# Gated linear attention: the values of two heads made in one product of 512 columns

## The reference

```
o_intra = where(causal, (q*exp(b)) @ (k*exp(-b)).T, 0) @ v     # by head and chunk
o_inter = (q*exp(b)) @ state;  state = decay*state + (k*exp(b_last-b)).T @ v
o = rmsnorm(o_intra + o_inter) * silu(r)
```

## Time and profile before

| what | value |
|---|---|
| median of 3 runs | 2038.2 us (2037.76 to 2039.65) |
| the profiled execution | 2040.08 us, of which 2038.0 us are the span from the first to the last instruction |
| PE busy | 99% of the span, 10,731 matmuls |
| DVE / ACT / GpSimd busy | 78% / 49% / 19% |
| granted clock of PE, mean | 0.997 |
| chain that ended last | PE 92%, DVE 5%, ACT 1% |

### The profile page before, as it was taken

One profiled execution on the slowest core, in us unless ns is written; L12 is line 12 of the kernel. 1 busy time (PEld: TensorE's weight loads), 2 busy tenths in 40 slices (PEclk: granted clock), 3 DMA queues, 4 the chain that ended last, 5 costly groups with the idle time before them and its releaser, 6 DMA issues.

```text
span 2038.0 us, 28513 instructions
## 1 busy us (share of the span) xinstructions
PE 2013.1 (99%) x10731; PEld 1766.3 (87%) x10731; DVE 1590.8 (78%) x2874; ACT 997.7 (49%) x1684; POOL 384.1 (19%) x298
## 2 busy tenths in 40 slices
PE   9999999999999999999999999999999999999998
PEld 7888888887887888889999999999998888888886
DVE  6799576757977455999898997777577888888886
ACT  6577455544245324434366767777343333333333
POOL 2000200000000001000122222222233444444430
PEclk9999999999999999999999999999999999999999
DMA  7411246341212222125789989999999999999991
GB/s 279 152 54 42 73 152 225 145 166 62 93 63 73 83 89 101 63 93 173 251 289 319 333 304 334 329 325 328 385 365 386 370 373 377 386 386 389 387 381 76
DMA packets 137288, 471.39 MB, mean 231 GB/s; under 512 B 10096, under 2 KB 59760, under 8 KB 111552
## 3 DMA queue, kind: packets, MB, share of 16 engines
q1 hardware_dynamic: 50368, 309.59, 41.4%
q0 software_dynamic: 36864, 134.23, 17.5%
q10 hardware_dynamic: 49920, 25.75, 4.3%
HBM read 416.97 MB, written 52.43 MB: 230 GB/s over the span
## 4 chain that ended last, share of the span: by engine, by line
PE 92%; DVE 5%; ACT 1%; issue 1%; DMA 0%; ACTq 0%; DVEq 0%
PE bank L159 91%; DVE whl L316 1%; DVE L L1593 1%; PE bank L756 1%; DVE L L1591 1%; PE bank L1688 0%; DVE L L1574 0%; PE bank L351 0%; DVE B L1063 0%; ACT whl L309 0%; DMA raw<-in_l_in 0%; DVE wk L2049 0%; DVE L L1979 0%; DVE i L2047 0%; DVE i L2055 0%
## 5 line engine op out<-in xcount | busy, mean ns | idle before, releaser
L159 PE MATMUL bank<-xhl,whl 128*128 128x384 f32 (+1 forms) x5256 | 1058.7, 359 | 8.2 <-DVE whl L316 3.2
L159 PEld LDWEIGHTS bank<-xhl,whl 128*128 128x128 f32 x5256 | 938.9, 189 | 92.2 <-issue 4.4
L316 DVE TENSOR_TENSOR whl<-raw,whl 128x1024 fp32r<-128x1024 f32 (+1 forms) x395 | 469.7, 1199 | 225.0 <-ACT whl L309 213.5
L309 ACT ACTIVATE whl<-raw 128x1024 fp32r<-128x1024 f32 (+1 forms) x395 | 400.7, 1027 | 258.6 <-PE bank L159 250.0
L159 PE MATMUL bank<-whl,ag 128*128 128x512 f32 x2304 | 525.3, 390 | 0.0
L159 PEld LDWEIGHTS bank<-whl,ag 128*128 128x128 f32 x2304 | 431.8, 188 | 89.3
L2406 POOL DMA_INDIRECT row<-in_U_rows,row_at x128 | 153.4, 1198 | 586.9 <-DVE row L2419 426.9
L2406 POOL DMA_INDIRECT row<-in_V_rows,row_at x128 | 186.5, 1457 | 245.7 <-DVE y_tok L2435 215.2
L2435 DVE SCALAR_TENSOR_TENSOR y_tok<-row,row_a,y_tok 128x1024 f32<-128x1024 f32 x127 | 162.5, 1280 | 2.6
L2419 DVE SCALAR_TENSOR_TENSOR row<-row,h_tok 128x1024 f32<-128x1024 f32 x128 | 155.8, 1218 | 3.0 <-DMA row<-in_U_rows,row_at 3.0
L159 PE MATMUL bank<-yhl,whl 128*128 128x512 f32 x636 | 149.6, 390 | 1.6 <-DVE whl L316 1.0
(11 more groups left out here) (300 smaller groups left out, 1834.7 us busy)
## 6 DMA issues: line engine op xcount, KB each, us to landing
raw<-in_U SPq DMA_DIRECT2D x64, 1024.0 KB, 7.4
raw<-in_V SPq DMA_DIRECT2D x64, 1024.0 KB, 7.5
hidden<-h_both SPq DMA_DIRECT2D x32, 768.0 KB, 10.4
gates<-g_stage ACTq DMA_DIRECT2D x12, 2048.0 KB, 24.8
g_ring<-gates SPq DMA_DIRECT2D x32, 768.0 KB, 12.5
h_ring<-hidden SPq DMA_DIRECT2D x22, 768.0 KB, 9.7
raw<-in_w_ada SPq DMA_DIRECT2D x16, 1024.0 KB, 5.6
raw<-in_w_gla SPq DMA_DIRECT2D x12, 1024.0 KB, 4.9
```

What stands on the lines that cost most here:

```text
L159: return e.matmul(o, a, b, start=start, stop=stop, skip_group_check=True)
L309: e.activation(hi[:, s], src[:, s], ACT.Copy).then_inc(act_hi.of((i, half)))
L316: e.tensor_tensor(lo[:, s], src[:, s], F(hi[:, s]), ALU.subtract).then_inc(dve_lo.of((i, half)))
```

## The change

Values are made for two heads at once, in P1 for heads 0 and 1 and in P3 for heads 2 and 3. A value item holds half the contraction (four chunks of X) for both heads' 512 columns, so that a pair takes two items (gla1 then gla4; gla7 then gla10), parts 0 and 1, and 96 matmuls of 512 columns. Four banks, one for each block of 128 tokens, are filled together ahead of the first matmul and stay open over both parts. P0 and P2 have no values. The order of items follows (`GLA_ITEMS`), and so do the splits. ACT copies a pair's values with eight copies of 256 columns.

Items from number 20 on (a = w_ada): before g0, g1, a, a, g3, g4, a, a, g2, a, a, g6, g7, a, a, g5, ...; after g0, a, a, g3, g1, g4, a, a, g2, a, a, g6, a, a, g5, a, a, g9, g7, g10, a, a, g8, a, a, g11.

```diff
+GLA_ITEMS = [(0,), (3, 1, 4), (2,), (6,), (5,), (9, 7, 10), (8,), (11,)]
...
+        def after_mix(h):
+            return IT["w_gla", 11] + 3 if h == 3 else IT["w_gla", (6, 9, 11)[h]]
...
 def tensor_gla ... first(h):                   # behind z
-                i += 1
-                hi, lo = hi_lo(i)
-                q.wait_ge(act_hi[i, 1], dve_lo[i, 1])
-                for half in range(2):
-                    b = gla_banks.fill(q, ("v", h, half))
-                    for qt in (2 * half, 2 * half + 1):
-                        for k in range(8):
-                            m = mul3(e, b[:, qt % 2 * 256:(qt % 2 + 1) * 256], X(k, qt * P, (qt + 1) * P),
-                                     (hi[:, k * 256:(k + 1) * 256], lo[:, k * 256:(k + 1) * 256]), qt % 2 == 0 and k == 0)
...
+                if h % 2 == 0:
+                    return
+                v = [gla_banks.fill(q, ("v", h, qt)) for qt in range(NT)]
+                for part, i in enumerate((IT["w_gla", 3 * h - 2], IT["w_gla", 3 * h + 1])):
+                    hi, lo = hi_lo(i)
+                    for qt in range(NT):
+                        for k in range(4):
+                            q.wait_ge(act_hi[i, k // 2], dve_lo[i, k // 2])
+                            o = k * 512
+                            m = mul3(e, v[qt], X(4 * part + k, qt * P, (qt + 1) * P), (hi[:, o:o + 512], lo[:, o:o + 512]),
+                                     part + k == 0, part == 1 and k == 3)
...
 def scalar_gla ...
-            split_hi(e, q, IT["w_gla", 0] + 1)
+            split_hi(e, q, IT["w_gla", 3])
... first(h):
-                if h > 0:
-                    split_hi(e, q, IT["w_gla", 3 * h] + 1)
+                if h == 3:
+                    split_hi(e, q, IT["w_gla", 7])
                 if h >= 2:
                     act_gla_root(e, q, h - 2)
                     act_gla_first(e, q, h - 2)
-                split_hi(e, q, IT["w_gla", 3 * h] + 4)
+                split_hi(e, q, IT["w_gla", (1, 4, 5, 10)[h]])
...
+                split_hi(e, q, IT["w_gla", 3 * h - 1])    # odd h, ahead of the copies of v
... mix(h):
-                split_hi(e, q, IT["w_gla", 3 * h + 2] + 3)
+                split_hi(e, q, after_mix(h))
 def vector_gla ... first(h):
-                split_lo(e, q, IT["w_gla", 3 * h] + 1)
+                if h == 0 or h == 3:
+                    split_lo(e, q, IT["w_gla", 3 if h == 0 else 7])
...
-                split_lo(e, q, IT["w_gla", 3 * h] + 4)
+                split_lo(e, q, IT["w_gla", (1, 4, 5, 10)[h]])
... behind k end, odd h:
+                    split_lo(e, q, IT["w_gla", 3 * h - 1])
```

More of the change, by code:

```diff
@@ L54 @@
         + [item for n, (what, h) in enumerate(GLA_STEPS)
-           for item in [("w_gla", 3 * h + j, ITEM) for j in (range(2) if what == "project" else (2,))]
+           for item in [("w_gla", j, ITEM) for j in GLA_ITEMS[n]]
            + [("w_ada", 8 + 2 * n + j, ITEM) for j in range(2)]]
@@ L1221, in first @@
                 gla_banks.give(("z", h), (dve_gla, ("z", h)))
-                i += 1
-                hi, lo = hi_lo(i)
-                q.wait_ge(act_hi[i, 1], dve_lo[i, 1])
-                for half in range(2):
-                    b = gla_banks.fill(q, ("v", h, half))
-                    for qt in (2 * half, 2 * half + 1):
-                        for k in range(8):
-                            m = mul3(e, b[:, qt % 2 * 256:(qt % 2 + 1) * 256], X(k, qt * P, (qt + 1) * P),
-                                     (hi[:, k * 256:(k + 1) * 256], lo[:, k * 256:(k + 1) * 256]), qt % 2 == 0 and k == 0)
-                    m.then_inc(pe_gla.of(("v", h, half)))
-                    gla_banks.give(("v", h, half), (act_gla, ("v", h, half)))
-                spent[i, 0] = spent[i, 1] = pe_gla, ("v", h, 1)
+                if h % 2 == 0:
[9 more added lines that the diff above has]
+                                     part + k == 0, part == 1 and k == 3)
+                        m.then_inc(pe_gla.of(("v", h, part, qt)))
+                    spent[i, 0] = spent[i, 1] = pe_gla, ("v", h, part, NT - 1)
+                for qt in range(NT):
+                    gla_banks.give(("v", h, qt), (act_gla, ("v", h, qt)))
             def mix(h):
@@ L1257, in mix @@
                     gla_root(e, q, 2)
-                q.wait_ge(act_gla["ke", h], act_gla["v", h, 1])
+                q.wait_ge(act_gla["ke", h], act_gla["v", h // 2 * 2 + 1, NT - 1])
                 for n in range(2):
@@ L1324, in first @@
                 e.activation(E3, E3, ACT.Exp, scale=1.0 / 16).then_inc(act_gla.of(("end", h)))
-                for half in range(2):
-                    q.wait_ge(pe_gla["v", h, half])
-                    copy(e, vtok[:, half * T:(half + 1) * T], gla_banks.of["v", h, half]).then_inc(act_gla.of(("v", h, half)))
+                if h % 2 == 0:
+                    return
+                split_hi(e, q, IT["w_gla", 3 * h - 1])
+                for qt in range(NT):
+                    q.wait_ge(pe_gla["v", h, 1, qt])
+                    for n in range(2):
+                        m = copy(e, gla_sets[n][5][:, qt * 256:(qt + 1) * 256], gla_banks.of["v", h, qt][:, n * 256:(n + 1) * 256])
+                    m.then_inc(act_gla.of(("v", h, qt)))
             def mix(h):
@@ L1367, in first @@
                                                ).then_inc(dve_out.of(("x1", k)))
-                dve_gla_ada(e, q, IT["w_gla", 3 * h] + 2)
+                dve_gla_ada(e, q, IT["w_gla", (0, 4, 6, 10)[h]] + 1)
                 if h >= 2:
                     dve_gla_recip(e, q, h - 2)
-                dve_gla_ada(e, q, IT["w_gla", 3 * h] + 3)
+                dve_gla_ada(e, q, IT["w_gla", (0, 4, 6, 10)[h]] + 2)
                 if h >= 2:
@@ L1400, in first @@
                 e.tensor_tensor(E3, gla_banks.of["k", h], E3, ALU.mult).then_inc(dve_gla.of(("k end", h)))
+                if h % 2 == 1:
+                    split_lo(e, q, IT["w_gla", 3 * h - 1])
             def mix(h):
@@ L1405, in mix @@
                     dve_gla_recip(e, q, 2)
-                split_lo(e, q, IT["w_gla", 3 * h + 2] + 3)
+                split_lo(e, q, after_mix(h))
                 dve_gla_ada(e, q, IT["w_gla", 3 * h + 2] + 1)
@@ L2884, in layouts @@
     r["w_gla"] = cols(w, ch)
-    r["w_gla"][1::3] = r["w_gla"][1::3].reshape(4, P, 2, 8, P).transpose(0, 1, 3, 2, 4).reshape(4, P, 2048)
+    values = r["w_gla"][1::3].reshape(2, 2, P, 2, 2, 4, P).transpose(0, 4, 2, 5, 1, 3, 6)
+    r["w_gla"][1::3] = values.reshape(4, P, 2048)
     for name, at, n in (("w_za", za, 1024), ("w_zb", zb, 1024), ("w_dkv", dkv, 256), ("w_iq", iq, 512),
```

## The result

The changed kernel takes 2056.1 us (median of 6 runs, 2055.0 to 2058.6) against 2038.3 for the kernel before on the same chip: ratio 1.0086, 95% interval 1.0076 to 1.0096. It is slower by 17.8 us. The profiled execution took 2058.55 us, the longest of the six; its span is 2056.6.

A forecast was written before the change was run, and what follows sets the result against it. PE was taken to bound the kernel. The terms -2.5 + 13.5 + 5.6 + 1.7 + 0.9 gave +19.2 us on the profiled 2040.1, so 2059.3, or 2057.4 as median (1.9 lower); range 2051 to 2063.

The forecast's parts named there:

- Step 1: v on PE: 192 matmuls of 512 columns at 229 ns replace four blocks of 96 narrower ones, 2.5 us gained.
- Step 2: P1, behind z of head 1: v waits for the bank that head 0's `k end` frees, 13.5 us lost.
- Step 3: M1, with P2 lacking values: r waits for g5's split and `u` for ACT's copy of `ke`, 5.6 us lost.
- Step 4: PE's clock: half clock costs 1.7 us after the P1 pause and 0.9 us at M1.
- Step 5: P3's values, ACT's eight copies and the splits cost nothing; no later PE idle stretch gives anything back.

The follow-up runs named there:

- e6: Changed kernel with every matmul of 512 value columns made as two of 256, 384 in all: 2059.8 us.
- e14: e13 with each matmul of 512 value columns made as two of 256: 2040.4 us, ratio 1.0004 to the kernel before.
- e1: Changed kernel with each of v's four banks filled just ahead of its first matmul, not all four together: 2051.9 us.
- e2: Changed kernel with g1 ahead of the two w_ada items in the order of loads: 2050.35 us.
- e9: Changed kernel with banks filled by block, head 0's q and k banks given back behind z's, DVE's g4 split and z before P1's w_ada items: 2047.4 us.
- e4: Changed kernel with g5 split at P2's start, ke and at copied before head 2's chain, head 1's state before g9's split and a w_ada item: 2056.3 us.
- e10: e4 with the banks of head 2's q and k also given back behind z's: 2055.95 us.
- e7: Changed kernel with 46 extra matmuls of 512 columns behind z of head 1, their result thrown away: 2054.6 us.
- e11: Changed kernel with e2's order of items and the edits of e9 and e10 together: 2041.6 us, ratio 1.0012 to the kernel before.
- e13: e11 with head 1's root and reciprocal ahead of g7's split in P3, and M1's two w_ada items behind the squares: 2039.1 us.

## Why the prediction was right

**Step 1** (gain 2.5): right. The wide matmul took 229 ns (21.94 us / 96), 2.6 us gained at full clock; e6's second pair (1.2 us more) and e14's first (1.24 more) confirm it from the other side. The Trainium skill's 131 ns ("TensorE: Matmul & The Clock Gate", section "Back-to-back issue gap") does not hold for these matmuls; the trace decides against it.

**Step 2** (13.5): the mechanism was right, shown by e1, e2 and e9; the size was 11.5, below the range of 12.7 to 15.3 given for it. `k end` ended at 305.9, not 308.0. g3 was issued 0.9 us earlier than taken, and g3 and g1 each landed 0.6 to 0.7 us sooner (4.8 and 4.9 us for 5.5). I took the bounds from the landing time of one load; two loads in a row and their common start move the sum. In e4, e6 and e10, which leave this stretch as it is, the gap is 12.6, 12.4 and 12.4 us, because PE comes to it up to 1.5 us earlier or `k end` ends up to 0.7 later; so one trace fixes its size to about 1 us only, and all four lie under the range.

**Step 3** (5.6): right to a tenth: from z's end to `u` 12.26 us (360.41 to 372.67), forecast 12.33, and 12.26 or 12.27 in e1, e2, e6 and e9 too, whose M1 is unedited. One part of the reason was incomplete: besides `ke`, `u` also waits for the bank of head 2's q, which ended 0.2 us earlier and so did not show.

**Step 4** (1.7 and 0.9): too low, 2.4 and 1.8, the second just over its bound of 1.7. The clock had already fallen in the pause and stayed at 0.50 for some 5 us of v. M1's 1.8 belongs to this execution: in e1, e2, e6 and e9 the clock fell already behind M1's first wait, where the wait for `ke` hides it, as the forecast had it, and only 0.1 us was lost behind `u`.

**Step 5**: right for P3's v, which follows z without a gap. That no later idle stretch gives anything back was wrong: the wait of 1.5 us in M3 brought the clock down (1.6 us), and the later one of 2.2 us spared as much. The errors, -2.0 on the stall and +1.6 on step 4's clock, nearly cancel, and so do these two. The mechanisms were right; that the sum, with 2057.4 forecast, came within 1.3 us is in part luck.

## What to carry to other kernels

Work that seems only slow may be the cover of other engines' chains: before a block of the bounding engine is moved, list every wait that ended inside it, and follow the rotation of buffers by number, since the wait moves to whoever now takes the late bank. Here each repair uncovered the next wait (a bank, then a reciprocal behind a split), and all of them together only brought the change back to no measurable difference: its gain was at most 2.6 us in 2038. A wait hidden under a later one costs nothing until the later one goes.

## What the runs showed of the hardware

A wait of the same length may or may not cost clock. The wait of 2.2 us of the earlier trace rows halved the clock in the kernel before and not in the changed one; the wait of 1.5 us in M3 did the reverse. Both waits stand in all twelve traces of this case, and the clock fell behind M3's in six of them (the changed kernel, e2, e4, e7, e9, e11), behind the one of 2.2 us in two (the kernel before, e10). By windows on PE, the kernel before, then the changed one, around the wait of 2.2 us:

```profile
936.00:940.00 4.00, 4.00 (x18) 0.66 0.54 156
```

```profile
956.00:960.00 4.00, 4.00 (x25) 1.00 0.45 139
```

Each such fall is worth about 1.6 us. What decides it these runs don't tell. That such falls also make the spread of 4 us over e13's runs was not tested, though the granted clock goes with it: 0.997 at 2036.6 to 2037.4 us (3 of 12), 0.995 or 0.996 at 2038.5 to 2040.5. At 0.997 the kernel before, measured beside it, took 2037.6 to 2038.7 (15 of 23), about 1 us more, as PE's timelines have it.
